# Scores against the compressed keys: both kv heads in one matmul, with the keys as a block diagonal

## What is computed

```
kcmp = compress_blocks(kc, w_pk, b_pk)                   # 31 blocks, 2 kv heads, 64
s_c = einsum('bqgrd,bngd->bqgrn', q * HEAD_DIM**-0.5, kcmp)
p_c = masked_softmax(s_c, (cmp_end[None, :] <= t[:, None]))
o_c = einsum('bqgrn,bngd->bqgrd', p_c, vcmp)
```

## Time and profile before

| | us |
|---|---|
| median of three runs | 987.77 |
| the three runs | 987.6, 987.77, 990.32 |
| the profiled execution, its own time | 990.21 |
| its span, first to last instruction | 988.6 |
| PE busy | 940.9 |
| DVE busy | 579.5 |
| ACT busy | 394.8 |
| POOL busy | 217.5 |

### The profile page before, as it was taken

One profiled execution on the slowest core, in us unless ns is written; L12 is line 12 of the kernel. 1 busy time (PEld: TensorE's weight loads), 2 busy tenths in 40 slices (PEclk: granted clock), 3 DMA queues, 4 the chain that ended last, 5 costly groups with the idle time before them and its releaser, 6 DMA issues.

```text
span 988.6 us, 17704 instructions
## 1 busy us (share of the span) xinstructions
PE 940.9 (95%) x6733; PEld 854.5 (86%) x6733; DVE 579.5 (59%) x1077; ACT 394.8 (40%) x719; POOL 217.5 (22%) x281
## 2 busy tenths in 40 slices
PE   4999999996999999899998999999999999999995
PEld 2899999996888878799786999999999997777774
DVE  4448688998556664467456566666666664113114
ACT  6211253544354544622244544455555543212112
POOL 6443242444433523132000011111111110000000
PEclk9999999998899999999999999999999999999998
DMA  7665542331200000262601222222222222232212
GB/s 218 137 189 187 127 100 71 105 87 43 51 23 2 23 23 28 59 182 87 159 26 43 65 85 85 85 82 73 79 85 85 85 85 85 68 98 69 81 64 95
DMA packets 110897, 84.58 MB, mean 86 GB/s; under 512 B 12978, under 2 KB 97850, under 8 KB 110776
## 3 DMA queue, kind: packets, MB, share of 16 engines
q1 hardware_dynamic: 104368, 65.64, 23.1%
q0 software_dynamic: 4048, 15.19, 5.5%
q10 hardware_dynamic: 2426, 2.98, 1.0%
HBM read 78.71 MB, written 7.18 MB: 87 GB/s over the span
## 4 chain that ended last, share of the span: by engine, by line
PE 88%; DVE 4%; ACT 3%; DMA 2%; issue 2%; POOL 1%; ACTq 0%; POOLq 0%; DVEq 0%; SPq 0%
PE ps L1585 25%; PE ps L1587 24%; PE ps L1586 24%; PE ps L1872 2%; PE ps L1849 2%; PE ps L1655 2%; PE ps L1809 1%; DVE yc L1230 1%; PE ps L1620 1%; DMA raw<-in_w_out_dram 1%; PE ps L1812 1%; DMA page<-in_state_kv_win_dram 1%; DVE wl L1161 1%; PE ps L1706 1%; PE ps L1815 1%
## 5 line engine op out<-in xcount | busy, mean ns | idle before, releaser
L1585 PE MATMUL ps<-z,wh 128*128 128x288 f32 x704 | 209.4, 297 | 3.3 <-DVE z L1490 3.3
L1586 PE MATMUL ps<-z,wh 128*128 128x288 f32 x704 | 208.3, 296 | 0.0
L1587 PE MATMUL ps<-z,wl 128*128 128x288 f32 x704 | 207.7, 295 | 0.0
L1161 DVE TENSOR_TENSOR wl<-raw,wh 128x1024 fp32r<-128x1024 f32 (+1 forms) x67 | 87.8, 1312 | 168.1 <-ACT wh L787 167.9
L787 ACT CAST wh<-raw 128x1024 fp32r<-128x1024 f32 (+1 forms) x67 | 69.6, 1040 | 274.9 <-PE ps L1587 261.6
L1585 PE MATMUL ps<-zh,wh 128*128 128x288 f32 (+1 forms) x560 | 175.3, 313 | 0.6 <-ACT g L942 0.5
L1586 PE MATMUL ps<-zl,wh 128*128 128x288 f32 (+1 forms) x560 | 166.7, 298 | 0.0
L1587 PE MATMUL ps<-zh,wl 128*128 128x288 f32 (+1 forms) x560 | 166.5, 297 | 0.0
L1585 PEld LDWEIGHTS ps<-z,wh 128*128 128x128 f32 x704 | 132.5, 188 | 3.7 <-issue 2.1
L1587 PEld LDWEIGHTS ps<-z,wl 128*128 128x128 f32 x704 | 133.3, 189 | 0.0
L1586 PEld LDWEIGHTS ps<-z,wh 128*128 128x128 f32 x704 | 132.8, 189 | 0.0
(11 more groups left out here) (282 smaller groups left out, 1578.3 us busy)
## 6 DMA issues: line engine op xcount, KB each, us to landing
raw<-in_w_up_dram SPq DMA_DIRECT2D x44, 512.0 KB, 3.8
raw<-in_w_in_dram SPq DMA_DIRECT2D x30, 512.0 KB, 3.9
raw<-in_w_down_dram SPq DMA_DIRECT2D x22, 512.0 KB, 3.6
page<-in_cache_kv_dram POOLq DMA_DIRECT2D x16, 256.0 KB, 3.0
raw<-in_w_out_dram SPq DMA_DIRECT2D x8, 512.0 KB, 3.7
x<-in_x_prompt_dram SPq DMA_DIRECT2D x4, 512.0 KB, 4.9
page<-in_state_kv_win_dram POOLq DMA_DIRECT2D x16, 128.0 KB, 2.9
raw<-in_w_in_dram SPq DMA_DIRECT2D x8, 256.0 KB, 3.5
```

The lines of the kernel that those rows point to most:

```text
L1161: nc.vector.tensor_tensor(wl[:, s % 2, 0:n], raw[:, s % 2, 0:n], wh[:, s % 2, 0:n].bitcast(F32), ALU.subtract).then_inc(lo_done, 1)
L1585: nc.tensor.matmul(out, ah, bh, start=start, stop=False)
L1586: nc.tensor.matmul(out, ah, bl, start=False, stop=False)
L1587: return nc.tensor.matmul(out, al, bh, start=False, stop=stop)
```

## The change

A new tile `kblk` of 128 partitions and 2 x 32 columns holds the prompt's compressed keys as a block diagonal: the keys of kv head 0 in partitions 0 to 63 and columns 0 to 30, those of kv head 1 in partitions 64 to 127 and columns 32 to 62, and zeros elsewhere. GpSimd clears it among its constants, and ScalarE copies the two blocks into it behind the compressed keys. `cmp_scores` then has four matmuls in place of eight, one for each r: the stationary side is `qT[:, r]` with all 128 partitions, the moving side the 64 columns of `kblk`. Each writes the scores of heads r and 4 + r side by side. The semaphore `cs_half` goes. VectorE's first operation reads PSUM in the order in which the heads now lie there (r, then g), and writes `sc` as before.

```diff
--- before.py
+++ after.py
@@ -313,6 +313,7 @@
         cgate = small("cgate", [P, HEADS])
         ptab = small("ptab", [1, NPG], I32)
         pT3 = at("pT3", [P, 512], F32, used[0])
+        kblk = at("kblk", [P, KVH, 32], F32, used[0] + 512)
         sfT = small("sfT", [P, 2 * FT, 2 * DB])
         pT_at = [pT[:, 0, :], pT[:, 1, :], pT[:, 2, :], pT3[:, :]]
         assert base + 4 * used[0] <= nc.sbuf_usable_end, (base + 4 * used[0], nc.sbuf_usable_end)
@@ -381,6 +382,7 @@
         win_out = sem("win_out")
         cmp_mm = sem("cmp_mm")
         cmp_ok = sem("cmp_ok")
+        kblk_ok = sem("kblk_ok")
         vc_t = sem("vc_t")
         vc_ok = sem("vc_ok")
         rsel_ok = sem("rsel_ok")
@@ -398,7 +400,6 @@
         pt_odd = sem("pt_odd")
         pt_half = sem("pt_half")
         pv_done = sem("pv_done")
-        cs_half = sem("cs_half")
         cs_full = sem("cs_full")
         cs_step = sem("cs_step")
         ce_in = sem("ce_in")
@@ -663,6 +664,7 @@
             fill(c01[:, :, :], 1.0)
             select(c01[:, :, :], ALU.is_ge, 0.0, 1 - CL, [[P, 4], [-CS, NCP]], 1)
             fill(phi[:, :, :], 0.0)
+            fill(kblk[:, :, :], 0.0)
             pool.wait_ge(pool_init, init[0])
             nc.gpsimd.memset(mean_w[:, :], 1.0 / CH).then_inc(const_ok, 1)
 
@@ -819,6 +821,12 @@
                     dst[:, NCP:].rearrange("p (b n) -> p b n", n=NCS),
                     ps[:, bk, SEQ // CS:SEQ // CS + DB * PAST // CS].rearrange("p (b n) -> p b n", b=DB)[:, :, 0:NCS],
                     ACT.Identity, bias=bphi[:, j:j + 1]).then_inc(cmp_ok, 1)
+                if j == 0:
+                    act.wait_ge(const_ok, 2)
+                    act.wait_ge(cmp_ok, 2)
+                    for g in range(KVH):
+                        rows = slice(g * HD, (g + 1) * HD)
+                        nc.scalar.copy(kblk[rows, g, 0:NCP], kcmp[rows, 0:NCP]).then_inc(kblk_ok, 1)
 
             def state_rows_out():
 
@@ -1242,8 +1250,9 @@
 
                 dve.wait_ge(cs_full, i + 1)
                 link(nc.vector.tensor_tensor(
-                    sc[:, :, :], ps[:, 7, 0:HEADS * 32].rearrange("p (h n) -> p h n", n=32)[:, :, 0:NCP],
-                    cneg[:, 3 - i, :].unsqueeze(1).broadcast_to([P, HEADS, NCP]), ALU.add))
+                    sc[:, :, :].rearrange("p (g r) n -> p g r n", g=KVH),
+                    ps[:, 7, 0:HEADS * 32].rearrange("p (r g n) -> p g r n", r=G, n=32)[:, :, :, 0:NCP],
+                    cneg[:, 3 - i, :].unsqueeze(1).unsqueeze(1).broadcast_to([P, KVH, G, NCP]), ALU.add))
                 link(nc.vector.tensor_reduce(cmax[:, :], sc[:, :, :], AX.X, ALU.max))
                 nc.vector.tensor_tensor(sc[:, :, :], sc[:, :, :],
                                         cmax[:, :].unsqueeze(2).broadcast_to([P, HEADS, NCP]),
@@ -1698,15 +1707,10 @@
                     pe.wait_ge(ln_xc, CT * i)
                 if i == 3:
                     pe.wait_ge(ln_step, 2)
-                for h in range(HEADS):
-                    g, r = h // G, h % G
-                    if h == G:
-
-                        pe.wait_ge(cs_half, i + 1)
-                    mm = nc.tensor.matmul(ps[:, 7, h * 32:h * 32 + NCP], qT[g * HD:(g + 1) * HD, r, q0:q0 + P],
-                                          kcmp[g * HD:(g + 1) * HD, 0:NCP], start=True, stop=True)
-                    if h == G - 1:
-                        mm.then_inc(cs_half, 1)
+                pe.wait_ge(kblk_ok, 2)
+                for r in range(G):
+                    mm = nc.tensor.matmul(ps[:, 7, r * 64:(r + 1) * 64], qT[:, r, q0:q0 + P],
+                                          kblk[:, :, :].rearrange("p g n -> p (g n)"), start=True, stop=True)
                 mm.then_inc(cs_full, 1)
 
             z = (zh, zl)
```

## The result

The changed kernel was run 20 times beside 20 runs of the kernel before: 986.24 us median (980.61 to 993.74) against 988.85 us (986.83 to 997.49). The ratio is 0.9959, with a 95% interval of 0.994 to 0.9977: 0.41% faster, 4.05 us on 988.85, the interval reaching from 2.3 to 5.9 us. The forecast was 3.6 us. The ratio is not that of the two medians: those are 2.61 us apart (0.9974), the means of the same runs (989.31 and 986.20) 3.1 us.

The account below looks back on a forecast made before the run. TensorE was taken to bound the kernel: three stages saving 0.85 us each and the first 1.02 sum to 3.57, say 3.6 us, off the 987.77 us median, giving 984.2 us; range 982.4 to 987.2 us.

Parts of the forecast that it names:

- What bounds the kernel: Whole kernel: TensorE, busy 940.9 of 988.6 us and holding 88% of the chain, is what others wait for in attention.
- The price of a pair, 0.11 us: New score stages: each load and matmul pair starts every 0.11 us, eight pairs a stage; other end 0.135 us.
- The gap of 0.20 us behind the block: After each stage's new matmuls: TensorE loses 0.20 us going from full-height to half-height shape, as after L1796.
- the front of the first stage: Ahead of stage one: the 0.16 us gap goes, since the block follows gate matmuls of the same full shape.
- The other parts: VectorE released 1.1 us earlier; ScalarE's copies (0.6 us) and GpSimd's memset (uncovered 0.4 us) covered by idle time.
- A: First stage: saving arrives and a half-clock spell behind it vanishes, worth 1.7 us more; 982.5 us, chance 0.13.
- The spell of the earlier trace: Kernel before, 258.36 to 261.77 us, behind the first stage: granted clock 0.50 with PE busy; rival A says it may vanish.
- B: Attention stages: the loop over maxima, exponentials and transposes sets the pace, so about half is lost; 986.0 us, chance 0.20.
- The stretch in which TensorE stands still: Near 360 to 370 us, PE busy 8.96 of 10: the gap follows work of the same stage and should move with it.
- C: Whole kernel: clock falls elsewhere once or twice, 1.7 us each, or scatter hides the saving; 987.8 us, chance 0.11.
- D: Score stages: each full-height load waits for the matmul before it, 0.46 us a pair; 995.4 us, chance 0.04.
- The chances of 0.58 and 0.37: Whole kernel time: 0.58 for faster by over 0.3% (below 984.8 us), 0.37 for within 0.3%.

Follow-up runs that it names:

- The preparation alone: Kernel before, with the block diagonal made (one more memset, two ScalarE copies) but not used, its eight matmuls unchanged; ratio 0.9996 to the kernel before.
- the execution above: One profiled execution of the unchanged change, run again to look for slow clock spells; mean granted clock 0.981, 989.24 us.
- The version with the first stage early: The change, with the first stage's four matmuls issued behind the first pair's scores, not two pairs later; 983.4 and 982.51 us, ratios 0.9939 and 0.992 to before.

## Why the prediction was right

**What bounds the kernel.** The intervals shrink by what a stage saves and grow by what one is charged (each matmul twice), to 0.01 us, and over the whole attention the four savings add up to the same 4.13 us. TensorE was the bound there.

**The price of a pair, 0.11 us.** Right: (0.97 - 0.19) / 7. The choice of the row with 31 columns over the one with 159 was right as well; 128 columns still fit under the load. The rule of the Trainium skill against it ("TensorE: Matmul & The Clock Gate", Part 3), by which the load would wait for the matmul on its own rows, does not hold in this kernel: the loads start every 0.11 us although each takes 0.19.

**The gap of 0.20 us behind the block.** This is the term that was mis-sized. It measured 0.07 us (292.97 to 293.04) and made the sum 0.5 us too small. I had taken it from the step behind the transposes as a fixed cost of changing the height. What is common to both places is something else: the next load starts shortly before the last matmul ends. Behind the block that matmul ends at 292.01 + 1.11 = 293.12, 0.08 us after the load began. Behind the transposes, in the kernel before:

```profile
304.62 0.62 PE L1796 MATMUL ps<-ident,sm 128*31 128x128 f32 x4
```

it ends at 305.24, 0.07 us after the load at 305.17. The loads of 31 columns there are short, so their last one ends long before its matmul; a load of 128 columns does not. The experiment with 128 moving columns agrees: its matmuls span 1.16 us and not 1.11, and the next load comes 0.05 us later. So do eight matmuls on all rows (they end at 292.87 + 1.97 = 294.84, the load begins at 294.77) and each matmul twice (296.02 and 295.95). The ends of matmul records are modelled, and no run changed this gap alone, so this is a reading that fits five places and not a cause that is shown. With 1.04 in place of 1.16 us for the block the sum 3.57 becomes 4.05, and the rows give 4.13; 0.06 of the rest is the front of the first stage, where 0.16 us of idle time stood for 0.22 between the starts of two loads.

**The other parts.** VectorE starts 1.15 us after the first load, 1.1 was said. ScalarE's two copies take 0.46 us together, and the idle time before the cast lost 0.69 with its waits, 0.6 was said. GpSimd's memset takes 0.15 us. The preparation alone came out at 0.9996, which leaves room for 1.4 us; "covered" is shown for the copies by the casts, 6.36 us apart before and 6.37 after, and for the memset it rests on the idle time behind it.

**The rivals.** *A* falls as a cause of this difference. The spell of the earlier trace rows is in none of the profiles of the change, but the kernel with the preparation alone, whose stages are those of before, has none at that place either. It has as much half speed in all, in one piece ahead of the first stage, from 240.7 to 254.3 us, where the kernel before has 241.3 to 251.6 and then the spell; of the five executions of the change one has the longer piece too (from 241.5 to 255.2), the others only some ten us. And the mean clock is 0.9841 in 44 runs (32 of the change, 12 with twice the columns) and 0.9843 in the 65 of before. *B* falls by the intervals, and only by them: the measured median, 986.24, lies nearer to its 986.0 than to the forecast. The stretch in which TensorE stands still moved with the rest, as was argued. First the kernel after, then the kernel before, 4.15 us later:

```profile
350.00:360.00 10.00, 8.81 (x88) 7.03 (x86) 8.40 (x20) 5.08 (x16) 3.51 (x5) 1.00 0.21 54
```

```profile
354.15:364.15 10.00, 8.81 (x88) 7.03 (x86) 8.40 (x20) 5.08 (x16) 3.53 (x5) 1.00 0.21 54
```

TensorE is busy for the same 8.81 of 10 us, and its idle time ahead of the output projection is 3.04 us in both. *C* is what single runs look like, not their ratio: the profiles before and after differ by 4.0 us in span, of which the first stretch up to the second stage gives 2.5 (57.43 to 54.95 us, with the spell of the earlier trace rows only before) and the last one takes back the fourth stage's saving (624.96 to 625.11 us, with one slow stretch more after 420 us in the profile after). Had I read only the two spans, I would have been right by accident. *D* falls with the spacing.

**The range and the chances.** The forecast of 984.2 us was made on a median of three runs, 987.77; with 20 it is 988.85, so the measured 986.24 lies above the forecast while the saving is larger than forecast. By the time itself the result fell into "within 0.3%" (984.8 was the border), by the ratio into "faster": 0.41%, with an interval that reaches down to 0.23%. The chances of 0.58 and 0.37 for the two don't look wrong, and more can't be said of them. That the time lay so well inside the range is partly luck; that the saving was 4.1 us for 3.6 said is not.

## What to carry to other kernels

A small float32 matmul here costs its load of 128 weight columns, 0.11 us for each of its two pairs, and up to 128 moving columns ride along. That it is the load's columns that count shows in the products with the values, which have 64 weight columns and 128 moving ones:

```profile
290.98 0.85 PEld L1876 LDWEIGHTS ps<-pT,ktok 128*64 128x64 f32 x16 [0.17 <-issue]
```

These loads, each 0.14 us long, start every (0.85 - 0.14) / 15 = 0.05 us. So fill the moving side and the rows with whatever shares the stationary operand, zeros included, and count pairs, not columns. Ask of such a block also where it stands: in an idle stretch of TensorE it costs nothing, and that needed one changed line for another 1.0 us. And where runs scatter by more than the effect, measure the distance between two landmarks of the program in the profile, in a stretch with the clock at full speed.

## What the runs showed of the hardware that was not expected

The granted clock falls to 0.50, the level of 1.2 GHz, for some 3.4 us at a time, twice in these executions for 6.8, while TensorE is busy (5.00 of 5 us from 478 to 483 in the execution above). In most cases it had stood idle for much of the time just before; but at 512.8 us it had been busy for 6.80 of the 6.80 us ahead, and ahead of the spell of the earlier trace rows for 3.35 of 3.41. In the 65 runs of the kernel before the time moves with the mean clock by some 0.9 us for each 0.001. One to five such stretches behind 400 us (the idle end of the program aside) were seen in profiled executions of kernels whose program is the same there. They lie at the same few places, near 410, 480 and 515 us and between 534 and 545, but which of them a run has differs, so it is not the program alone that decides.

The version with the first stage early had a mean clock of 0.9873 in both of its series, on two chips, and never one under 0.985 in 13 runs; the 32 runs of the change reach down to 0.976. Its program differs only before 260 us, and the further half-speed stretches of a longer run lie behind 400 us. How the one could lead to the other stays open, and so does whether it does: the 12 runs with each matmul twice had 0.9865 with the stage in its old place. What its advantage has over 5 us therefore rests on an observation that repeated once, not on a cause that is known.
